# First norm of a decoder layer: POOL applies the norm's weights, VectorE the reciprocal column

## The chip, the cores and the metric

The kernel runs on one core of one Trainium2 chip. The metric is the device time in microseconds of that core, from runs of the whole program. The core's engines are called as in the profile: PE (TensorE), DVE (VectorE), ACT (ScalarE), POOL (GpSimd), and SP (SyncE), which issues all the DMAs here.

## What is computed

One layer of a decoder on 1024 tokens of width 1024 with 16 meta tokens in front (1040 rows in all), float32. Cut to what matters here:

```python
def rms_norm(x, g):
    y = xf * lax.rsqrt(jnp.mean(xf * xf, axis=-1, keepdims=True) + RMS_EPS)
    return (y * g.astype(jnp.float32)).astype(x.dtype)

mix = hybrid_mixer(rms_norm(h, g_mix_pre[l]), w_in[l], ...)
h = h + rms_norm(mix, g_mix_post[l])
ff = sq_relu_mlp(rms_norm(h, g_mlp_pre[l]), w_mlp_in[l], w_mlp_out[l])
h = h + rms_norm(ff, g_mlp_post[l])
```

The mixer projects the normalised rows with `w_in` and runs two kinds of attention on the result (stick-breaking attention and a sparse one in which an indexer picks 256 keys), gates and merges both, and projects out. The change concerns the first `rms_norm` alone, the one with `g_mix_pre`.

## The kernel before

All products of matrices are split: each operand is kept as a rounded part (`_hi`) and the rest (`_lo`), and three matmuls stand for one. The program has three blocks, one behind the other (the `nc.Block()` of lines 331, 506 and 1281). Each block holds a stream of instructions for every engine, and at its end all five engines meet in a barrier: nothing of the next block begins before all have arrived. The first block is the first norm, the second the projections and both attentions, the third the branches, the output projection and the MLP.

In the first block the 1040 rows are cut into nine tiles of 128 rows (`NT` is 9; the last has `LAST`, 16 rows). SP loads tile 0 of `x` (two DMAs), then the weights `g_bc` (one row, broadcast to 128 partitions), tile 1, the identity `idf`, and the other tiles, with the first two units of projection weights (`w_raw`) in between. For each tile c, with s = c % 2:

- ACT `first(c)` squares the tile with a sum per row (line 364, `junk1` and `small`) and, when DVE has made the variance, takes the square root (line 366).
- DVE `first(c)` makes the variance (line 388), the reciprocal of the root (line 390), and the normalised tile `xn[s]` (line 393), one SCALAR_TENSOR_TENSOR: `x` times the reciprocal column times `g_bc`. From tile 2 on it waits for the transposes of tile c - 2, which read the same half of `xn`. Ahead of everything DVE waits for `g_bc`.
- PE transposes `xn` in eight pieces into `tps[s]`, 128x128 each (line 419), when DVE has read the tile before last out of it.
- ACT `second(c)` rounds `tps` into `x_hi` (line 371), DVE `second(c)` subtracts that from `tps` into `x_lo` (line 399).

ACT and DVE both go `first(0)`, then `first(c)` and `second(c-1)` for c from 1 to 8, then `second(8)`; the order is written out by hand, and each engine executes in that order. ACT moreover casts the weight units 0 and 1 to `w_hi` (line 303) behind `second(4)` and `second(6)`. POOL does nothing in this block but `rest_unit` (line 307): `w_lo` from `w_raw` and `w_hi`, once for each of the two units. At the end DVE makes two small casts (lines 407, 408).

All sizes of `xn`, `xs`, `g_bc` and `x_lo` are 1024 columns of float32 per partition. The later blocks are named here only where a row comes from them: line 307 again (weights), line 630 and 639 (POOL, rests of projections and of transposed attention weights), lines 654 and 1345 (POOL, an addition of two tiles and `w_lo` in the third block), lines 1072, 1093 and 1102 (DVE, TENSOR_SCALARs of the search for the 256 keys), line 1119 (DVE, a product of two tiles), line 1578 (DVE, a square), line 683 (PE, the projections).

Of the kernel before, what the change touches and what calls it, by code (L numbers as in the profile page):

```python
# [16 lines left out]
F32, F32R, BF16, I32 = mybir.dt.float32, mybir.dt.float32r, mybir.dt.bfloat16, mybir.dt.int32  # L17
ALU, ACT = mybir.AluOpType, mybir.ActivationFunctionType
ds = bass.ds

P = 128
D = 1024
# [10 lines left out]
NT = -(-T // P)  # L33
# [147 lines left out]
for m_ in range(HI * NCH):  # L181
    n_, k_ = slots_[m_ * len(slots_) // (HI * NCH)]
# [48 lines left out]
O_SEL = O_XA + 2 * KT * T * 4  # L231
# [16 lines left out]
def build(nc, x, meta, w_units, b_gate, g_pre, g_post, g_mlp_pre, g_mlp_post, ident, strict, fill,  # L248
          rope_i, rope_d, out):
    with ExitStack() as ctx:  # L250
        def at(name, shape, dt, off):
            return nc.alloc_sbuf_tensor_at(name, shape, dt, offset=off)

        def sem(name):
            return ctx.enter_context(nc.semaphore(name))

        def psum(stack, name, shape):
            return stack.enter_context(nc.psum_tensor(name, shape, F32))
# [26 lines left out]
        small = at("small", [P, 512], F32, O_CONST + 2560)  # L285
# [14 lines left out]
        def round_unit(act, v, s, use):  # L300

            act.wait_ge(raw_landed[s], (use + 1) * 16)
            act.copy(w_hi[:, s], w_raw[:, s]).then_inc(hi_done, 1)  # L303

        def rest_unit(pool, v, s):
            pool.wait_ge(hi_done, v + 1)
            pool.tensor_tensor(w_lo[:, s], w_raw[:, s], w_hi[:, s].bitcast(F32), ALU.subtract).then_inc(lo_done, 1)  # L307
# [14 lines left out]
        xs = at("xs", [P, NT, D], F32, O_SEL)  # L322
        xn = at("xn", [P, 2, D], F32, O_SEL + NT * D * 4)
        g_bc = at("g_bc", [P, D], F32, O_SEL + NT * D * 4 + 8192)
        junk1 = at("junk1", [P, D], F32, O_SEL + NT * D * 4 + 12288)
        with ExitStack() as st:  # L326
            tps = [psum(st, f"n_tps{i}", [P, KT, P]) for i in range(2)]
            const_in, id_in, g_in, sq_done, var_done, std_done, r_done = (sem("n_" + n) for n in ("const", "id", "g", "sq", "var", "std", "r"))
            x_in = [sem(f"n_x{c}") for c in range(NT)]
            xn_done, t_done, h_done, l_done, cast_done = (sem("n_" + n) for n in ("xn", "t", "hi", "lo", "cast"))  # L330
            block = st.enter_context(nc.Block())

            def rows(c):
                return LAST if c == NT - 1 else P

            @block.sync
            def _(sp):
                def load_x(c):
                    if c == 0:
                        sp.dma_start(xs[0:META, 0], meta).then_inc(x_in[0], 16)  # L340
                        sp.dma_start(xs[META:P, 0], x[0:P - META, :]).then_inc(x_in[0], 16)
                    else:
                        sp.dma_start(xs[0:rows(c), c], x[c * P - META:c * P - META + rows(c), :]).then_inc(x_in[c], 16)

                load_x(0)
                sp.dma_start(g_bc[:], g_pre.broadcast_to([P, D])).then_inc(g_in, 16)
                load_x(1)
                sp.dma_start(idf[:], ident).then_inc(id_in, 16)
                for c in range(2, NT):
                    load_x(c)  # L350
                    if c in (3, 5):
                        v = (c - 3) // 2
                        sp.dma_start(w_raw[:, v], w_units[v * P:(v + 1) * P, :].rearrange("p (k n) -> p k n", k=KT)).then_inc(raw_landed[v], 16)
                for t, src in ((fill_f, fill), (strict_f, strict), (bg, b_gate)):
                    sp.dma_start(t[:], src).then_inc(const_in, 16)

            @block.scalar
            def _(act):
                act.activation(small[:, 30:31], nc.const_aps.tensor(1.0, (P, 1), F32), ACT.Sqrt)

                def first(c):
                    r, s = rows(c), c % 2
                    act.wait_ge(x_in[c], 32 if c == 0 else 16)
                    act.activation(junk1[0:r], xs[0:r, c], ACT.Square, accum_out=small[0:r, s:s + 1]).then_inc(sq_done, 1)
                    act.wait_ge(var_done, c + 1)
                    act.activation(small[0:r, 4 + s:5 + s], small[0:r, 2 + s:3 + s], ACT.Sqrt).then_inc(std_done, 1)

                def second(c):
                    r, s = rows(c), c % 2
                    act.wait_ge(t_done, c + 1)  # L370
                    act.copy(x_hi[:, :, c * P:c * P + r], tps[s][:, :, 0:r]).then_inc(h_done, 1)

                first(0)
                for c in range(1, NT):
                    first(c)
                    second(c - 1)
                    if c in (5, 7):
                        round_unit(act, (c - 5) // 2, (c - 5) // 2, 0)
                second(NT - 1)

            @block.vector
            def _(dve):
                dve.wait_ge(g_in, 16)

                def first(c):
                    r, s = rows(c), c % 2
                    dve.wait_ge(sq_done, c + 1)
                    dve.tensor_scalar(small[0:r, 2 + s:3 + s], small[0:r, s:s + 1], 1.0 / D, EPS, ALU.mult, ALU.add).then_inc(var_done, 1)
                    dve.wait_ge(std_done, c + 1)
                    dve.reciprocal(small[0:r, 6 + s:7 + s], small[0:r, 4 + s:5 + s]).then_inc(r_done, 1)  # L390
                    dve.wait_ge(r_done, c + 1)
                    dve.wait_ge(t_done, c - 1) if c >= 2 else None
                    dve.scalar_tensor_tensor(xn[0:r, s], xs[0:r, c], small[0:r, 6 + s:7 + s], g_bc[0:r], ALU.mult, ALU.mult).then_inc(xn_done, 1)

                def second(c):
                    r, s = rows(c), c % 2
                    cols = slice(c * P, c * P + r)
                    dve.wait_ge(h_done, c + 1)
                    dve.tensor_tensor(x_lo[:, :, cols], tps[s][:, :, 0:r], x_hi[:, :, cols].bitcast(F32), ALU.subtract).then_inc(l_done, 1)

                first(0)
                for c in range(1, NT):
                    first(c)
                    second(c - 1)
                second(NT - 1)
                dve.wait_ge(const_in, 48)
                dve.tensor_copy(strict_b[:], strict_f[:]).then_inc(cast_done, 1)
                dve.tensor_copy(idb[:], idf[:]).then_inc(cast_done, 1)

            @block.tensor  # L410
            def _(pe):
                pe.wait_ge(id_in, 16)
                for c in range(NT):
                    r, s = rows(c), c % 2
                    pe.wait_ge(xn_done, c + 1)
                    if c >= 2:
                        pe.wait_ge(l_done, c - 1)
                    for kt in range(KT):
                        mm = pe.transpose(tps[s][:, kt, 0:r], xn[0:r, s, kt * P:(kt + 1) * P], idf[0:r, 0:r])
                    mm.then_inc(t_done, 1)  # L420

            @block.gpsimd
            def _(pool):
                for v in range(2):
                    rest_unit(pool, v, v)

# [37 lines left out]
        with ExitStack() as st:  # L464
# [363 lines left out]
            def _(act):  # L828
# [30 lines left out]
                def relu(m):  # L859
                    _, c0, c1 = CH[m % NCH]  # L860
                    act.wait_ge(s_ready, m + 1)
                    if m >= 4:
                        act.wait_ge(s_acc, m - 3)
                    act.activation(relu_b[:, m % 4, 0:c1 - c0], bk[2 + m % 4][:, 0:c1 - c0], ACT.Relu).then_inc(s_relu, 1)
# [399 lines left out]
        with ExitStack() as st:  # L1264
# [14 lines left out]
            x_in = [sem("t_x0"), sem("t_x1")]  # L1279
# [400 lines left out]
```

## Time and profile before

| | us |
|---|---|
| median of 3 runs | 1809.07 (1806.93 to 1817.53) |
| profiled execution | 1808.41 |
| its span, first to last instruction | 1806.6 |
| PE busy | 1713.6 (95%) |
| DVE busy | 1009.9 (56%) |
| ACT busy | 690.9 (38%) |
| POOL busy | 546.0 (30%) |

The granted clock of TensorE is 0.99 of full speed over the whole span. A row of the timeline begins with the start and the duration in microseconds; an instruction that is held up after its issue shows the wait as part of its duration. In square brackets stands how long the engine was idle before, and what ended that.

### The profile page before, as it was taken

The page shows a single profiled execution, that of the slowest core. Times are in us where ns is not written, and L with a number is a line of the kernel's source. Part 1 is how long each engine was busy: PE and PEld are TensorE (multiplying, and loading weights), DVE is VectorE, ACT ScalarE, POOL GpSimd, SP SyncE. Part 2 cuts the span into 40 slices and gives each one's busy share as a digit, 9 for nine tenths or more (in the row PEclk, how much of TensorE's full clock was granted, in tenths as well). Part 3 has the DMA queues.
Part 4 walks back from the last instruction along what each step waited for, and adds up shares of the span by engine and source line. Part 5 has one row for each costly group of instructions (what it writes and reads, how often), then busy time and mean ns, then how long its engine had stood idle before and what let it go on. Part 6 is the DMA issues. An engine that isn't in the chain of part 4 may idle for free.

```text
span 1806.6 us, 22857 instructions
## 1 busy us (share of the span) xinstructions
PE 1713.6 (95%) x8744; PEld 1446.5 (80%) x8744; DVE 1009.9 (56%) x1626; ACT 690.9 (38%) x1356; POOL 546.0 (30%) x281
## 2 busy tenths in 40 slices
PE   5989999999999999888899999999999999999998
PEld 4889888899877777777778788888888888888886
DVE  5277798798898899678744344222222222222225
ACT  5366555554554544677621324111212020303032
POOL 1112255563443444211024501222223130404033
PEclk9999899999999999999999999999999999999999
DMA  4565424534424323644134431211111111202023
GB/s 169 159 176 158 124 91 128 148 97 113 120 71 110 113 87 93 144 106 108 41 140 152 175 117 71 70 36 58 47 47 49 46 59 35 74 20 82 12 86 136
DMA packets 67044, 174.56 MB, mean 97 GB/s; under 512 B 9256, under 2 KB 23912, under 8 KB 66936
## 3 DMA queue, kind: packets, MB, share of 16 engines
q1 hardware_dynamic: 66936, 173.10, 31.3%
q8 instruction: 70, 1.15, 0.3%
q14 instruction: 38, 0.31, 0.1%
HBM read 128.57 MB, written 44.50 MB: 96 GB/s over the span
## 4 chain that ended last, share of the span: by engine, by line
PE 47%; POOL 1%; DVE 1%; DMA 1%; ACT 0%; issue 0%; DVEq 0%
PE bank L1368 22%; PE bank L1393 19%; PE bank L317 5%; POOL row_lo L1345 1%; DMA w_raw<-w_units 1%; PE bank L1386 0%; DVE nn L1571 0%; POOL w_lo L307 0%; DVE scaled L1603 0%; DVE tt L1553 0%; ACT L1483 0%; DVE hh L1558 0%; DVE acc L1591 0%; DVE fin L1608 0%; DVE m_lo L1562 0%; ACT nn L1489 0%
## 5 line engine op out<-in xcount | busy, mean ns | idle before, releaser
L683 PE MATMUL bk<-x_hi,w_hi 128*128 128x512 f32 (+2 forms) x832 | 309.1, 372 | 1.2 <-PEq L326 1.2
L683 PE MATMUL bk<-x_lo,w_hi 128*128 128x512 f32 (+2 forms) x832 | 299.1, 360 | 0.0
L683 PE MATMUL bk<-x_hi,w_lo 128*128 128x512 f32 (+2 forms) x832 | 298.6, 359 | 0.0
L1496 ACT ACTIVATE relu<-bank 128x1024 f32<-128x1024 f32 x32 | 32.9, 1029 | 504.8 <-PE bank L1393 504.8
L1345 POOL TENSOR_TENSOR w_lo<-w_raw,w_hi 128x1024 fp32r<-128x1024 f32 x32 | 82.9, 2599 | 397.9 <-ACT w_hi L1460 397.9
L1393 PE MATMUL bank<-m_hi,w_hi 128*128 128x512 f32 x512 | 199.5, 390 | 0.0
L1393 PE MATMUL bank<-m_hi,w_lo 128*128 128x512 f32 x512 | 199.2, 389 | 0.0
L1393 PE MATMUL bank<-m_lo,w_hi 128*128 128x512 f32 x512 | 199.2, 389 | 0.0
L639 POOL TENSOR_TENSOR pt_lo<-a_buf,pt_hi 128x512 fp32r<-128x512 f32 (+3 forms) x104 | 138.3, 1347 | 193.0 <-ACT pt_hi L903 192.9
L307 POOL TENSOR_TENSOR w_lo<-w_raw,w_hi 128x1024 fp32r<-128x1024 f32 x53 | 130.4, 2461 | 191.6 <-ACT w_hi L303 191.4
L1060 DVE TENSOR_SCALAR_CACHE_REDUCE counted<-sc,small 128x272 uint8<-128x272 f32 (+6 forms) x217 | 182.4, 890 | 0.9
L1591 DVE TENSOR_TENSOR acc<-acc,bank 128x1024 f32<-128x1024 f32 x56 | 68.4, 1221 | 192.5 <-PE bank L1368 191.7
L683 PEld LDWEIGHTS bk<-x_hi,w_lo 128*128 128x128 f32 x832 | 158.6, 191 | 17.6
L683 PEld LDWEIGHTS bk<-x_hi,w_hi 128*128 128x128 f32 x832 | 159.1, 191 | 16.0 <-issue 1.3
L683 PEld LDWEIGHTS bk<-x_lo,w_hi 128*128 128x128 f32 x832 | 159.1, 191 | 13.5
L1578 DVE TENSOR_TENSOR sq<-relu 128x1024 f32<-128x1024 f32 x32 | 39.2, 1225 | 227.9 <-ACT relu L1496 227.9
L783 PE MATMUL bk<-pt_hi,v_hl 128*128 128x256 f32 (+2 forms) x384 | 110.9, 313 | 10.6 <-ACT o_st L922 5.8
L1393 PEld LDWEIGHTS bank<-m_hi,w_lo 128*128 128x128 f32 x512 | 96.1, 188 | 20.0
L1393 PEld LDWEIGHTS bank<-m_lo,w_hi 128*128 128x128 f32 x512 | 96.1, 188 | 19.9
L1393 PEld LDWEIGHTS bank<-m_hi,w_hi 128*128 128x128 f32 x512 | 96.1, 188 | 19.8
L748 PE MATMUL bk<-idf,a_buf 128*128 128x128 f32 (+1 forms) x704 | 100.3, 277 | 4.1 <-DVE pt_lo L1165 2.5
L1116 DVE TENSOR_TENSOR_SCAN n_buf<-n_buf 128x1040 f32<-128x1040 f32 (+3 forms) x64 | 101.8, 1591 | 2.3 <-ACT n_buf L879 2.3
(187 smaller groups left out, 3461.7 us busy)
## 6 DMA issues: line engine op xcount, KB each, us to landing
w_raw<-w_units SPq DMA_DIRECT2D x99, 512.0 KB, 3.6
raw<-w_units SPq DMA_DIRECT2D x24, 512.0 KB, 3.3
k_hi<-k_d SPq DMA_DIRECT2D x32, 260.0 KB, 5.7
k_lo<-k_d SPq DMA_DIRECT2D x32, 260.0 KB, 6.2
q_st<-q_d SPq DMA_DIRECT2D x32, 256.0 KB, 4.9
g_d<-stage_hi SPq DMA_DIRECT2D x32, 256.0 KB
gate<-g_d SPq DMA_DIRECT2D x16, 512.0 KB, 4.5
qi<-iq_d SPq DMA_DIRECT2D x32, 128.0 KB, 3.1
```

The costliest lines, as they stand in the source:

```text
L307: pool.tensor_tensor(w_lo[:, s], w_raw[:, s], w_hi[:, s].bitcast(F32), ALU.subtract).then_inc(lo_done, 1)
L317: mm = pe.matmul(o, w[:, s, kt, :], a[:, a_of(kt), c0:c1], start=(kt == kts[0] and n == 0), stop=(kt == kts[-1] and n == 2))
L639: pool.tensor_tensor(pt_of(pt_lo, j, tiles), raw, pt_of(pt_hi, j, tiles).bitcast(F32), ALU.subtract).then_inc(sb_lo, 1)
L683: mm = pe.matmul(pj[b][:, 0:c1 - c0], w[:, s, kt, :], a[:, kt, c0:c1], start=kt == 0 and k == 0, stop=kt == KT - 1 and k == 2)
L748: mm = pe.transpose(bk[TP_BANK[n]][0:r, m * P:(m + 1) * P], a_buf[:, j % 3, col:col + r], idf[:])
L783: mm = pe.matmul(dst, v_hl[0:r, g % 2, slot, :], w[0:r, cols], start=slot == 0 and w is hi, stop=slot == o + 1 and w is lo)
L1060: op(dve.tensor_scalar(counted[:, blk(b)], sc[:, blk(b)], cand[:, j:j + 1], None, ALU.is_ge, ALU.add, accum_out=cnt[:, j:j + 1]))
L1116: dve.tensor_tensor_scan(n[:, ::-1], n[:, ::-1], n[:, ::-1], 1.0, ALU.mult, ALU.bypass).then_inc(scan_done, 1)
L1345: pool.tensor_tensor(unit_lo(v), raw_ring[(v - V0) % 3], unit_hi(v).bitcast(F32), ALU.subtract).then_inc(lo_done, 1)
L1368: mm = pe.matmul(ps[:, c * HALF:(c + 1) * HALF], a[:, cols], w[:, c * HALF:(c + 1) * HALF], start=first and n == 0, stop=last and n == 2)
L1393: mm = pe.matmul(m1_ps[n][:, c * HALF:(c + 1) * HALF], w[s][:, kt, :], a[:, kt, c * HALF:(c + 1) * HALF], start=kt == 0 and i == 0, stop=k ...
L1591: dve.tensor_tensor(acc[:, t], acc[:, t], m2_ps[g][:], ALU.add).then_inc(acc_done, 1)
```

## The change

POOL gets a new instruction per tile: `xg[c % 3] = x[c] * g_bc`, into a ring of three buffers of 128x1024 that lies behind `junk1`. It waits for `g_bc` once, for the tile's load, and from tile 3 on for DVE's `xn` of tile c - 3, which reads the same buffer. DVE's product becomes a TENSOR_SCALAR, `xg` times the reciprocal column; it waits for POOL's product besides what it waited for, and DVE no longer waits for `g_bc`. POOL's two `rest_unit` stand behind its nine products.

```diff
@@ -323,11 +323,12 @@
+        xg = at("xg", [P, 3, D], F32, O_SEL + NT * D * 4 + 16384)
...
-            xn_done, t_done, h_done, l_done, cast_done = (sem("n_" + n) for n in ("xn", "t", "hi", "lo", "cast"))
+            xg_done, xn_done, t_done, h_done, l_done, cast_done = (sem("n_" + n) for n in ("xg", "xn", "t", "hi", "lo", "cast"))
@@ -380,8 +381,6 @@
             @block.vector
             def _(dve):
-                dve.wait_ge(g_in, 16)
-
                 def first(c):
@@ -389,8 +388,9 @@
                     dve.wait_ge(r_done, c + 1)
+                    dve.wait_ge(xg_done, c + 1)
                     dve.wait_ge(t_done, c - 1) if c >= 2 else None
-                    dve.scalar_tensor_tensor(xn[0:r, s], xs[0:r, c], small[0:r, 6 + s:7 + s], g_bc[0:r], ALU.mult, ALU.mult).then_inc(xn_done, 1)
+                    dve.tensor_scalar(xn[0:r, s], xg[0:r, c % 3], small[0:r, 6 + s:7 + s], None, ALU.mult).then_inc(xn_done, 1)
@@ -421,6 +421,13 @@
             @block.gpsimd
             def _(pool):
+                pool.wait_ge(g_in, 16)
+                for c in range(NT):
+                    r = rows(c)
+                    pool.wait_ge(x_in[c], 32 if c == 0 else 16)
+                    if c >= 3:
+                        pool.wait_ge(xn_done, c - 2)
+                    pool.tensor_tensor(xg[0:r, c % 3], xs[0:r, c], g_bc[0:r], ALU.mult).then_inc(xg_done, 1)
                 for v in range(2):
                     rest_unit(pool, v, v)
```

POOL's instructions in the first block, before (`n_...` and `hi_done` are semaphores; `n_x0` to `n_x8` count the loads of `x`, `n_g` that of `g_bc`, `n_xn` DVE's products):

```order
L422 UNCONDITIONAL_BRANCH [waits barrier_Pool_Activation_PE_DVE_SP_gather]
L307 ISA
L307 TENSOR_TENSOR w_lo<-w_raw,w_hi 128x1024 [waits hi_done] x2
L326 UNCONDITIONAL_BRANCH
L623 UNCONDITIONAL_BRANCH [waits barrier_Pool_Activation_PE_DVE_SP_gather]
```

and of the changed kernel:

```order
L430 ISA
L430 TENSOR_TENSOR xg<-xs,g_bc 128x1024 [waits n_x0,n_g]
L430 TENSOR_TENSOR xg<-xs,g_bc 128x1024 [waits n_x1]
L430 TENSOR_TENSOR xg<-xs,g_bc 128x1024 [waits n_x2]
L430 TENSOR_TENSOR xg<-xs,g_bc 128x1024 [waits n_xn,n_x3]
L430 TENSOR_TENSOR xg<-xs,g_bc 128x1024 [waits n_xn,n_x4]
L430 TENSOR_TENSOR xg<-xs,g_bc 128x1024 [waits n_xn,n_x5]
L430 TENSOR_TENSOR xg<-xs,g_bc 128x1024 [waits n_xn,n_x6]
L430 TENSOR_TENSOR xg<-xs,g_bc 128x1024 [waits n_xn,n_x7]
L430 TENSOR_TENSOR xg<-xs,g_bc 16x1024 [waits n_xn,n_x8]
L307 TENSOR_TENSOR w_lo<-w_raw,w_hi 128x1024 [waits hi_done] x2
```

Nine products now stand ahead of the two `w_lo`; the one-off set-up (`ISA`) has moved to the first of them.

DVE's first instructions of the block, before (`n_sq` counts ACT's sums, `n_std` its roots, `n_r` the reciprocals, `n_hi` the rounded tiles):

```order
L388 TENSOR_SCALAR small<-small 128x1 [waits n_sq,n_g]
L390 RECIPROCAL small<-small 128x1 [waits n_std]
L393 SCALAR_TENSOR_TENSOR xn<-xs,small,g_bc 128x1024 [waits n_r]
L388 TENSOR_SCALAR small<-small 128x1 [waits n_sq]
L390 RECIPROCAL small<-small 128x1 [waits n_std]
L393 SCALAR_TENSOR_TENSOR xn<-xs,small,g_bc 128x1024 [waits n_r]
L399 TENSOR_TENSOR x_lo<-n_tps,x_hi 128x8x128 [waits n_hi]
```

and of the changed kernel (`n_xg` counts POOL's products):

```order
L387 TENSOR_SCALAR small<-small 128x1 [waits n_sq]
L389 RECIPROCAL small<-small 128x1 [waits n_std]
L393 TENSOR_SCALAR xn<-xg,small 128x1024 [waits n_xg,n_r]
L387 TENSOR_SCALAR small<-small 128x1 [waits n_sq]
L389 RECIPROCAL small<-small 128x1 [waits n_std]
L393 TENSOR_SCALAR xn<-xg,small 128x1024 [waits n_xg,n_r]
L399 TENSOR_TENSOR x_lo<-n_tps,x_hi 128x8x128 [waits n_hi]
```

The order on DVE is the same; the wait for the weights has gone from the first instruction, and each product waits for POOL's.

## Rows read from the trace of the kernel before

**Rows 1.** Stretches: PE, PEld, DVE, ACT, POOL busy (count); granted clock, DMA share, GB/s.

```profile
38.54:1806.60 1768.06, 1696.90 (x8672) 1433.00 (x8672) 984.94 (x1588) 668.01 (x1316) 541.06 (x275) 0.99 0.31 95
```

**Rows 2.** Who waited for whom from 0 to 45 us: total, times, longest.

```profile
PE n_tps L419 <- DVE xn L393: 20.6, 9, 9.0
```

**Rows 3.** Timeline, the start of the stage: start us, duration us, engine, line.

```profile
6.98 0.15 DVE L388 TENSOR_SCALAR small<-small 128x1 f32<-128x1 f32 x1 [6.98 <-DMA g_bc<-g_pre]
...
7.61 1.28 DVE L393 SCALAR_TENSOR_TENSOR xn<-xs,small,g_bc 128x1024 f32<-128x1024 f32 x1
...
8.30 1.06 ACT L364 ACTIVATE junk<-xs 128x1024 f32<-128x1024 f32 x1 [0.92 <-DMA xs<-x]
```

**Rows 4.** Timeline, from `xn` of tile 3 to `xn` of tile 5.

```profile
16.76 1.28 DVE L393 SCALAR_TENSOR_TENSOR xn<-xs,small,g_bc 128x1024 f32<-128x1024 f32 x1
...
18.10 1.97 PE L419 MATMUL n_tps<-idf,xn 128*128 128x128 f32 x8 [0.98 <-DVE xn L393]
...
19.95 1.28 DVE L393 SCALAR_TENSOR_TENSOR xn<-xs,small,g_bc 128x1024 f32<-128x1024 f32 x1
...
21.15 1.22 DVE L399 TENSOR_TENSOR x_lo<-n_tps,x_hi 128x1024 fp32r<-128x1024 f32 x1
...
22.90 1.28 DVE L393 SCALAR_TENSOR_TENSOR xn<-xs,small,g_bc 128x1024 f32<-128x1024 f32 x1
```

**Rows 5.** Timeline, the stage's second part, where POOL works too.

```profile
24.34 1.23 DVE L399 TENSOR_TENSOR x_lo<-n_tps,x_hi 128x1024 fp32r<-128x1024 f32 x1 [0.16 <-ACT x_hi L371]
...
25.34 2.35 POOL L307 TENSOR_TENSOR w_lo<-w_raw,w_hi 128x1024 fp32r<-128x1024 f32 x1 [24.89 <-ACT w_hi L303]
...
26.34 0.15 DVE L388 TENSOR_SCALAR small<-small 128x1 f32<-128x1 f32 x1 [0.77 <-ACT junk L364]
...
26.96 1.81 DVE L393 SCALAR_TENSOR_TENSOR xn<-xs,small,g_bc 128x1024 f32<-128x1024 f32 x1
...
30.43 1.28 DVE L393 SCALAR_TENSOR_TENSOR xn<-xs,small,g_bc 128x1024 f32<-128x1024 f32 x1
...
34.46 1.83 DVE L393 SCALAR_TENSOR_TENSOR xn<-xs,small,g_bc 16x1024 f32<-16x1024 f32 x1
...
37.71 0.29 DVE L399 TENSOR_TENSOR x_lo<-n_tps,x_hi 128x128 fp32r<-128x128 f32 x1 [0.29 <-ACT x_hi L371]
```

**Rows 6.** Prices elsewhere: DVE line 1072 by shape; POOL line 654, ns min/median/max.

```profile
L1072 DVE TENSOR_SCALAR sc<-sc,small 128x1040 f32<-128x1040 f32 x1 | 0.8, 752 | 0.0
...
L654 POOL TENSOR_TENSOR o_raw<-o_raw,o_raw x4: 2362/2374/2379, 748.9 to 835.6; 128x1024 f32<-128x1024 f32 x4
```

**Rows 7.** Timeline of the search: two TENSOR_SCALARs and the POOL instructions they met.

```profile
675.61 3.14 POOL L307 TENSOR_TENSOR w_lo<-w_raw,w_hi 128x1024 fp32r<-128x1024 f32 x1
676.51 2.65 DVE L1102 TENSOR_SCALAR sc<-sel_tmp 128x784 f32<-128x784 f32 x1
...
696.99 3.02 POOL L639 TENSOR_TENSOR pt_lo<-a_buf,pt_hi 128x512 fp32r<-128x512 f32 x2 [2.31 <-ACT pt_hi L903]
...
698.78 1.79 DVE L1093 TENSOR_SCALAR sel_tmp<-sel_tmp,small 128x1040 f32<-128x1040 f32 x1
```

**Rows 8.** Timeline: both engines wait at 241 to 244; POOL waits for VectorE at 1200.

```profile
241.47 3.06 DVE L1119 TENSOR_TENSOR a_buf<-a_buf,n_buf 128x784 f32<-128x784 f32 x1
...
241.30 2.40 POOL L307 TENSOR_TENSOR w_lo<-w_raw,w_hi 128x1024 fp32r<-128x1024 f32 x1 [4.36 <-ACT w_hi L303]
243.64 1.75 POOL L639 TENSOR_TENSOR pt_lo<-a_buf,pt_hi 128x384 fp32r<-128x384 f32 x1
...
1198.86 1.23 DVE L1578 TENSOR_TENSOR sq<-relu 128x1024 f32<-128x1024 f32 x1 [10.72 <-ACT relu L1496]
1199.84 2.51 POOL L1345 TENSOR_TENSOR w_lo<-w_raw,w_hi 128x1024 fp32r<-128x1024 f32 x1 [49.83 <-ACT w_hi L1460]
```

**Rows 9.** Busy time by stretch, columns as in rows 1: the second block's first matmuls.

```profile
38.50:44.20 5.70, 5.61 (x19) 5.64 (x20) 0.00 (x0) 0.00 (x0) 0.00 (x0) 1.00 0.78 274
44.20:46.00 1.80, 1.80 (x12) 1.80 (x12) 0.00 (x0) 0.69 (x2) 0.00 (x0) 1.00 0.06 25
```

## The prediction

> **What bounds the kernel now.** I read the table of stretches first. The stage that the change touches, the first norm, lasts from the start to 38.54 us. In the 1768.06 us behind it TensorE is busy for 1696.90, 96% [rows 1]. All five engines leave the stage through a barrier, and all later work starts behind that, so I take a change of the stage's length to pass to the total one for one: TensorE is the limit there and nothing in it waits for a time of day. The whole stage is 2% of the span; no edit to it can move the total by much, and 1% (18 us, about what a measurement of this kernel can tell from no change) is half the stage.
>
> Next the waits of that stretch: TensorE waited 20.6 us for `xn`, the product that is changed [rows 2]. So the path goes through VectorE. Then the timeline. At the start VectorE waits for the weights `g_bc` (6.98) and multiplies tile 0 at 7.61 [rows 3]. In the steady part the tiles run as two chains, even and odd ones. The odd chain in [rows 4]: `xn` of tile 3 at 16.76, its transposes at 18.10, ScalarE's rounding behind them, VectorE's `x_lo` at 21.15, and, behind the small work for the reciprocal, `xn` of tile 5 at 22.90. That is 6.14 us for two tiles, 3.07 per tile. Without the multiplication itself (1.28) it is 22.90 - 18.04 = 4.86 us from the end of one `xn` to the moment when the next of that chain can start.
>
> **What the change removes.** Nine products of 1.28 us on VectorE become nine TENSOR_SCALARs with one tile as input. The same form with a column as factor stands in the later search: 128x1040 in 0.752 us [rows 6], so about 0.74 for 1024 columns. If only that counted, 0.54 us would go from each two-tile chain, 0.27 per tile, some 2.2 us over eight tiles.
>
> **What it adds.** Nine POOL multiplications 128x1024 (the last with 16 partitions, as long, since length goes by columns: VectorE's `xn` of 16 partitions took 1.83, that of 128 under the same conditions 1.81 [rows 5]). The trace has no POOL multiplication. Its additions of the same shape and type took 2.362 to 2.379 us [rows 6], and I take 2.37. Bounds: from 2.0 (a multiplication somewhat cheaper than an addition) to 3.0, between the addition and the 3.14 of a subtraction that was held up [rows 7]. POOL is idle in the stage before, save for two `w_lo` of 2.35, so its 21.3 us of work have room; what matters is when it runs and whom it blocks.
>
> **What it collides with.** In the stage of before `xn` of tile 6 took 1.81 instead of 1.28 where it met POOL's `w_lo`: POOL ended at 25.34 + 2.35 = 27.69, VectorE at 28.77, 1.08 later. Tile 8 paid the same [rows 5]. The new form does this too: the TENSOR_SCALAR of 676.51 had to take 0.6 and took 2.65; POOL ended at 678.75, VectorE at 679.16. With 1040 columns, the one at 698.78 ended at 700.57, 0.56 after POOL (700.01) [rows 7]. So a `xn` that meets a running multiplication stands still until POOL is through and then needs 0.55 us. Instructions that read PSUM do not: `x_lo` at 24.34 ran over POOL's start at 25.34 with neither longer, and the small L388 at 26.34 (0.15) under POOL neither [rows 5].
>
> Who gets on when both wait? At 241.30 POOL ran a `w_lo` until 243.70 and had its next instruction issued at 243.64; VectorE had been waiting since 241.47. VectorE went first (it ended at 244.53, 0.83 after the release, the length of 784 columns), and POOL's 128x384 ended at 245.39, having taken 1.75. Behind VectorE's product that ended at 1200.09, POOL's 128x1024 ended at 1202.35, 2.26 later [rows 8]. So the two take turns, at 0.56 + 2.27 = 2.83 us per tile. The Trainium skill says so too (SBUF — State Buffer, section "Who interferes with whom"): a VectorE instruction in a mode that uses both port pairs, as a float32 `tensor_scalar` can be, and a GpSimd instruction exclude each other for their whole length. Its advice, to put the contended work off the critical path, speaks against this change: the product is on the path, and its feeder now holds it up. The trace agrees with the exclusion; on the turn when both queue, the page is silent.
>
> **The sum, tile by tile** (ends of `xn`):
> - Tile 0. POOL: 6.98 to 9.35. It issues the next at 9.30 (0.06 before an end, as at 243.64; x of tile 1 is there, ScalarE reads it at 8.30 [rows 3]). VectorE, told of the product, asks at 9.39, 0.09 late, and waits for the whole second multiplication: until 11.67, end 12.22. Before: 8.89. So +3.3.
> - Tile 1. The third multiplication runs 12.22 to 14.49. `xn` is asked for at about 12.8, waits, and ends at 15.04.
> - Tiles 2 to 5: one every 2.83, so tile 5 ends at 12.22 + 5 x 2.83 = 26.37. Before: 22.90 + 1.28 = 24.18. So +2.2; 1.1 of 3.3 has come back. The two-tile chain would allow it: 2 x 2.83 - 0.55 = 5.11 is more than 4.86.
> - Tile 6. ScalarE casts a weight in between, so it is asked for 26.96 - 21.23 = 5.73 after tile 4's end (23.54), at 29.27 (21.23 is 1.28 behind the start at 19.95 [rows 4]). Behind tile 5's end POOL makes its eighth multiplication until 28.64 and goes straight on with the last, until 30.97, since nothing is queued against it at that moment; `xn` waits for it and ends at 31.52. Before 28.77: +2.75. POOL's `w_lo` of unit 0 queues behind it, to 33.79.
> - Tile 7: asked for 1.66 after tile 6's end (30.43 - 28.77), at 33.18, waits for `w_lo`, ends 34.34. Before 31.71: +2.6.
> - Tile 8: asked for 5.69 after tile 6's end, 37.21. The second `w_lo` starts about 35.6 (its cast follows the rounding of tile 6), ends about 38.0; `xn` ends 38.55. Before 34.46 + 1.83 = 36.29: +2.3. The last `x_lo` moves from 37.71 [rows 5] to 40.0, and with it the barrier.
>
> The profiled execution took 1808.41 us (span 1806.6 and 1.8 around it), 0.7 below the median of the three runs, 1809.07. It gives 1810.7 with +2.3, the median 1811.4. I take 1811.0.
>
> **What is left uncertain in it.** Each 0.1 us on POOL's multiplication moves eight turns, some 0.8 us. With 2.6 it is +4; with 2.2 or less the two-tile chain takes over at (4.86 + 0.55)/2 = 2.7 per tile, and it is +1 to +2. TensorE's rate in the next stage is another term: its first matmuls there took 5.61 us for 19, 0.295 each; those behind 44.2 us 1.80 for 12, 0.15 each, of the same shape, while the granted clock reads 1.00 in both stretches [rows 9]. So 19 matmuls cost 0.145 more, some 2.8 us in all. Whether that stretch stays as long when the stage before it has other gaps, no row tells; I take no change, and -2.8 to +2.8 as its ends.
>
> **Rivals.**
> 1. *No exclusion in this pairing: faster.* If `xn` did not stand still beside POOL's multiplication, tile 0 would end at 9.39 + 0.74 = 10.13 (+1.2), and each pair of tiles would take 6.14 - 0.54 = 5.60. Over eight tiles that is -2.2, and tiles 6 and 8 lose the 0.5 that they wait for `w_lo` now: about -1.8 in all, 1807. It decides as soon as `xn` takes 0.74 rather than 0.9 or more at tiles 2 to 5. For it: the sharing is in the trace only with POOL subtractions and additions. Against it: both TENSOR_SCALARs that started while POOL ran stood until POOL's end, and so did a product of two tiles (241.47) [rows 7, 8]. 0.12.
> 2. *POOL goes on first whenever both queue.* Then three multiplications run before tile 0 (end 14.0, `xn` 14.5, +5.6), the ring is full, and each turn has the semaphore's 0.04 and an unshortened 2.37: 2.96. With the two `w_lo` also ahead, tile 8 ends near 41.6: +5.3, 1813.9. For it: POOL issues back to back. Against: the turn at 243.70. 0.12.
> 3. *A POOL multiplication is slower than an addition.* At 3.0 us, 0.63 more in nine turns: +2.3 + 5.7 = +8, 1816. No row speaks for or against. 0.08.
> 4. *TensorE's slower stretch moves* by up to its whole length: 1808.2 or 1813.8. 0.08.
>
> **How the numbers follow.** The forecast has 0.60. The range for 8 in 10 reaches from rival 1 (1807) to short of rival 3: 1807 to 1815.5; three runs of the kernel before lie 10 us apart, so the high side is left wide. A difference above 18 us is reached by no case: faster 0.01, slower 0.02, within 1% 0.97.
>
> **What would show it.** In the changed kernel's timeline: `xn` of tile 0 with about 2.8 us instead of 0.74; `xn` of tiles 2 to 5 with 0.8 to 0.9, ending 2.8 apart; POOL's multiplications with 2.4 twice and then about 2.9, back to back; the last `x_lo` near 40. Wrong: `xn` at 0.74 throughout (rival 1); three multiplications ahead of the first `xn` (rival 2); POOL rows of 3 us with nothing before them (rival 3); a stage that is longer and a total that isn't, or the reverse (rival 4).

## The result and the profile after

| | before | after |
|---|---|---|
| median | 1809.9 us (22 runs, 1805.25 to 1817.53) | 1817.79 us (22 runs, 1810.07 to 1823.57) |
| ratio to before | | 1.0040, 95% interval 1.0027 to 1.0054 |
| ratio in a second comparison (12 runs, with other kernels beside it) | | 1.0021, interval 1.0005 to 1.0036 |
| profiled execution, span | 1808.41, 1806.6 | 1814.99, 1813.1 |
| start of the second block | 38.59 | 43.71 |

The changed kernel is slower, by 0.4% in the first comparison and 0.2% in the second. The forecast was 1811.0 with a range to 1815.5: the sign was right, the size too small by more than half, and the median lies outside the range. The first block, where the change is, takes 5.12 us longer; 2.3 had been worked out.

The timeline of the changed kernel's first block, VectorE's product `xn`, tile by tile (start us, duration us; tiles 0, 1, 2, 3, 6, 7 and 8). These are the rows that answer to [rows 3 to 5]:

```profile
9.35 2.73 DVE L393 TENSOR_SCALAR xn<-xg,small 128x1024 f32<-128x1024 f32 x1 [2.26 <-POOL xg L430]
...
12.62 2.23 DVE L393 TENSOR_SCALAR xn<-xg,small 128x1024 f32<-128x1024 f32 x1
...
17.01 2.91 DVE L393 TENSOR_SCALAR xn<-xg,small 128x1024 f32<-128x1024 f32 x1
...
21.58 1.39 DVE L393 TENSOR_SCALAR xn<-xg,small 128x1024 f32<-128x1024 f32 x1
...
31.74 2.68 DVE L393 TENSOR_SCALAR xn<-xg,small 128x1024 f32<-128x1024 f32 x1
...
36.09 0.75 DVE L393 TENSOR_SCALAR xn<-xg,small 128x1024 f32<-128x1024 f32 x1
...
40.11 1.30 DVE L393 TENSOR_SCALAR xn<-xg,small 16x1024 f32<-16x1024 f32 x1
```

Tile 7 shows the price of the new form with nothing in its way: 0.75, where [rows 3] have 1.28. All others wait in place. The first two are as forecast (9.39 and 2.83; 12.8, end 15.04). Tile 2 is where the run leaves the forecast: it took 2.91, to 19.92, not to 17.9. POOL's rows of the same stretch (its products of tiles 2, 3, 4, 5 and 8, then the first `w_lo`) say why:

```profile
11.49 2.80 POOL L430 TENSOR_TENSOR xg<-xs,g_bc 128x1024 f32<-128x1024 f32 x1
14.26 2.81 POOL L430 TENSOR_TENSOR xg<-xs,g_bc 128x1024 f32<-128x1024 f32 x1
17.02 2.34 POOL L430 TENSOR_TENSOR xg<-xs,g_bc 128x1024 f32<-128x1024 f32 x1
...
20.06 2.36 POOL L430 TENSOR_TENSOR xg<-xs,g_bc 128x1024 f32<-128x1024 f32 x1 [0.70 <-DVE xn L393]
...
29.22 2.35 POOL L430 TENSOR_TENSOR xg<-xs,g_bc 16x1024 f32<-16x1024 f32 x1 [0.69 <-DVE xn L393]
31.54 2.33 POOL L307 TENSOR_TENSOR w_lo<-w_raw,w_hi 128x1024 fp32r<-128x1024 f32 x1
```

The products of tiles 2 and 3 took 2.80: 0.04 until the product before them was through, 0.55 for the `xn` in front, then 2.21 of their own. The next was issued at 17.02, `xn` of tile 2 at 17.01, and the product that both waited for ended at 17.07. POOL went on, and `xn` waited for all of it. This near miss is called the race of tile 2 below. With that product POOL had filled three buffers and could not issue the next product until `xn` had freed one: the rows from 20.06 on begin 0.14 behind an `xn`'s end, after 0.7 of idleness. From there a tile costs 3.05 (20.06, 23.11, 26.16), the pace of before, and none of the late start comes back. Last, `w_lo` went in at 31.54, 0.20 ahead of `xn` of tile 6, which cost that tile 1.9 us more than the 0.75 of a free product. The waits of the first 45 us carry the sum; the first answers to [rows 2] (20.6 there):

```profile
PE n_tps L419 <- DVE xn L393: 25.7, 9, 12.2
...
POOL xg L430 <- DVE xn L393: 2.8, 4, 0.7
DVE small L389 <- ACT small L367: 2.4, 9, 0.3
DVE xn L393 <- POOL xg L430: 2.3, 1, 2.3
```

TensorE waits 5.1 us longer for `xn`. VectorE waited for POOL's result itself only once, for tile 0; the rest of its loss is inside the durations above, where no view of waits shows it.

### The profile page after: what moved, and what is told of

It reads as the page before. It is cut to its first block, busy times and chain, and to the rows that moved or that the text cites. A ratio compares the mean times of both kernels' runs of the same rounds, so it can differ in the third digit from the quotient of the medians.

```text
span 1813.1 us, 22874 instructions
## 1 busy us (share of the span) xinstructions
PE 1713.8 (95%) x8744; PEld 1446.4 (80%) x8744; DVE 1013.6 (56%) x1626; ACT 690.8 (38%) x1356; POOL 568.1 (31%) x290
## 4 chain that ended last, share of the span: by engine, by line
PE 47%; POOL 1%; DVE 1%; DMA 1%; ACT 0%; issue 0%; DVEq 0%
PE bank L1375 22%; PE bank L1400 19%; PE bank L317 5%; POOL row_lo L1352 1%; DMA w_raw<-w_units 1%; PE bank L1393 0%; DVE nn L1578 0%; POOL w_lo L307 0%; DVE tt L1560 0%; DVE scaled L1610 0%; ACT L1490 0%; DVE hh L1565 0%; DVE acc L1598 0%; DVE m_lo L1569 0%; DVE fin L1615 0%; ACT nn L1496 0%
```

## Experiments

Theory A was what the rows above suggest: the loss is the exclusion between POOL's product and VectorE's, and its size depends on who is in front at each turn. Theory B, the rival: POOL as a feeder is too slow or too late, and the exclusion is a side show. Most runs are one profile each; what is compared is the start of the second block (TensorE's first matmul there), which repeats (43.71 and 43.52 for the changed kernel in two sessions, 41.74 and 41.81, 40.92 and 40.99, 39.25 and 39.12 for three of the others), while totals move by 10 us.

### Fewer buffers, and more

```diff
...
-        xg = at("xg", [P, 3, D], F32, O_SEL + NT * D * 4 + 16384)
+        xg = at("xg", [P, 1, D], F32, O_SEL + NT * D * 4 + 16384)
...
-                    if c >= 3:
-                        pool.wait_ge(xn_done, c - 2)
+                    if c >= 1:
+                        pool.wait_ge(xn_done, c - 0)
```

> One buffer instead of three: POOL starts a product only when xn of the tile before is through. Theory A (the loss comes from POOL going ahead and holding xn up, made worse by the race lost at tile 2): with one buffer POOL can't be in front of a waiting xn, so xn takes 0.75 at tiles 0 to 5, a tile costs 2.34 + 0.75 + 0.08 = 3.17, and the second block starts at 40.5, 3.2 us before that of the changed kernel (43.7), though the overlap is less. Rival B (POOL's throughput as a feeder is the limit, the exclusion is a side show): fewer buffers can only cost; the second block starts at 43.7 or later, up to 9 x 3.17 behind the start, no earlier than after.

The second block started at 41.74, 2.0 earlier than with three buffers. The timeline of VectorE and POOL at tiles 3 and 8, with the second `w_lo` in a row of its own:

```profile
19.43 0.75 DVE L393 TENSOR_SCALAR xn<-xg,small 128x1024 f32<-128x1024 f32 x1 [0.97 <-POOL xg L430]
...
36.17 2.82 DVE L393 TENSOR_SCALAR xn<-xg,small 16x1024 f32<-16x1024 f32 x1 [0.28 <-POOL xg L430]
...
38.34 2.86 POOL L307 TENSOR_TENSOR w_lo<-w_raw,w_hi 128x1024 fp32r<-128x1024 f32 x1
```

`xn` took 0.75 at tiles 0 to 7, and a tile cost 3.35 (3.17 expected: each handing over by semaphore took 0.11 to 0.14, not the 0.04 that I had put in). At the end the two `w_lo` and the last `xn` met, as the 2.82 shows. The last `w_lo` ended at 41.20, and VectorE's small cast of line 407 stood behind it (0.67 us, 0.22 before). Both the longer turn and this meeting make it 41.74 instead of 40.5. Theory B is wrong here: a third of the buffers and less overlap gave a shorter stage. Timed later, it came to a ratio of 1.0015:

> The kernel with one buffer again, timed in rounds. Its second block started at 41.74, 3.15 after that of before and 1.97 before that of the changed kernel, so the total is 3.2 us over before (0.17%), if the stage is all that differs; the clock of the later stages moves single runs by up to 10 us either way.

Measured 1813.44 against 1809.72 (12 and 23 runs), ratio 1.0015, interval 1.0001 to 1.0029; 3.2 us are 1.0018.

With nine buffers and no wait:

> Nine buffers, no wait of POOL for VectorE at all. Theory A: POOL still goes first where xn is asked for a hair late, so some xn take 2.9 and the second block starts at 43 to 44.5, no better than with three buffers (only if the race at tile 2 is won by chance, 40.6). Rival B: with its waits gone (0.7 before each product from tile 5 on) POOL delivers sooner; the second block starts near 41 or earlier.

It started at 42.75, 0.25 under A's range, far from B's 41, and 1.0 before the changed kernel. `xn` of tile 2 lost the race again, at 17.07 against POOL's 17.09, and from there the two took turns, as I had forecast for three buffers:

```profile
17.07 2.93 DVE L393 TENSOR_SCALAR xn<-xg,small 128x1024 f32<-128x1024 f32 x1
...
21.66 1.10 DVE L393 TENSOR_SCALAR xn<-xg,small 128x1024 f32<-128x1024 f32 x1
...
24.86 0.75 DVE L393 TENSOR_SCALAR xn<-xg,small 128x1024 f32<-128x1024 f32 x1
```

So the full ring costs about 1 us of the 5.1; the late start of tile 0, the lost race and `w_lo` make the rest. POOL's waits alone, as in B, do not explain it.

### One wait more

```diff
                     if c >= 3:
-                        pool.wait_ge(xn_done, c - 2)
+                        pool.wait_ge(xn_done, 3 if c == 4 else c - 2)
```

> Three buffers, and one wait more: POOL's product of tile 4 waits for xn of tile 2. Theory A: the race of 17.0 us goes the other way, xn of tile 2 takes 0.75 instead of 2.9 and ends near 17.8 (19.92 after); what follows can lose a race elsewhere, so the second block starts between 40.4 and 41.9, 2 to 3 us earlier, by one added wait. Rival B: an added wait can only delay POOL: 43.7 or later.

It started at 40.92, 2.8 earlier. VectorE's row for tile 2:

```profile
17.09 0.75 DVE L393 TENSOR_SCALAR xn<-xg,small 128x1024 f32<-128x1024 f32 x1
```

An added wait on one POOL instruction gave back more than half of the stage's loss. This is the sharpest test of the race: all instructions and buffers are the same. What is left against before is 2.33 us, the 2.3 of the forecast's sum, and it comes about tile by tile as forecast: `xn` of tile 6 waited for POOL's last product (2.25 at 29.38; 29.27 and 2.25 forecast) and that of tile 8 ended at 38.62 (38.55 forecast). Timed:

> One wait more at tile 4, as in the earlier run (second block at 40.92). Stage alone: 2.3 us over before, ratio 1.0013, and 2.8 under the changed kernel beside it. Rival C: 5 over before.

1811.6 us, ratio 1.0009, interval 0.9993 to 1.0025: not told apart from before.

### A slower product that holds nothing up

```diff
-                    dve.tensor_scalar(xn[0:r, s], xg[0:r, c % 3], small[0:r, 6 + s:7 + s], None, ALU.mult).then_inc(xn_done, 1)
+                    dve.tensor_scalar(xn[0:r, s], xg[0:r, c % 3], small[0:r, 6 + s:7 + s], None, ALU.mult, ALU.add,
+                                      accum_out=small[0:r, 8 + s:9 + s]).then_inc(xn_done, 1)
```

> VectorE's product also writes a sum to an unused column, the form that ran at POOL's side unstretched in the search. Everything else as in the changed kernel. Theory A: xn takes 1.27 to 1.35 at all nine tiles though its own work has nearly doubled, POOL's products 2.34 to 2.36 each with none at 2.8; the second block starts at 39.8, 3.9 us earlier than with the form that takes 0.75. Rival B: xn is slower by 0.5 and POOL as before: 43.7 or later.

Start 39.25, 4.5 earlier than the changed kernel. By line, over all nine tiles (ns min/median/max):

```profile
L431 POOL TENSOR_TENSOR xg<-xs,g_bc x9: 2342/2357/2375, 7.1 to 26.3; 128x1024 f32<-128x1024 f32 x8, 16x1024 f32<-16x1024 f32 x1
...
L393 DVE TENSOR_SCALAR_CACHE_REDUCE xn<-xg,small x9: 1268/1279/1280, 9.6 to 35.7; 128x1024 f32<-128x1024 f32 x8, 16x1024 f32<-16x1024 f32 x1
```

Neither engine shows a single stretched instruction. VectorE's own work on the product went from 0.75 to 1.28 and the stage got shorter. That settles that the exclusion, and not POOL's speed or the dependency, makes the loss. The Trainium skill has both halves (SBUF — State Buffer, section "Who interferes with whom"): a `tensor_scalar` can take the shared ports, "not the form that also writes out its accumulator". The trace agrees: 1.27 to 1.28 at every tile, beside POOL products of 2.34 to 2.38. Timed:

> The product in the form with a sum (second block at 39.25 in the earlier run). Stage alone: 0.7 us over before, ratio 1.0004, no difference that can be told; rival C, where it is POOL's added work or its heat that costs the later blocks: 3 to 4 over before.

1809.34 us, ratio 0.9993, interval 0.9977 to 1.0008, that is 4.2 us less to 1.4 more than before. The stage's 0.7 is inside, the 3 to 4 of rival C are not: POOL's nine products cost the later blocks nothing that this comparison can tell.

### The two halves apart

VectorE's half: `xn` from `x` itself, POOL's products gone; the norm's weights are left out.

> VectorE's half alone: xn is x times the reciprocal column; POOL makes no products, and the norm's weights are left out of the result. Theory A: 0.75 at most tiles, 1.2 at the two that meet w_lo; the second block starts at 36.6, 2.0 earlier than before (38.59). So the shorter form by itself is worth 2 us, and POOL's half costs 7 (36.6 to 43.7). Rival B agrees on this run; a start at 38 or later would say that VectorE's product was never on the path.

Start 35.66, 2.9 earlier than before. (0.9 earlier than estimated; the product of tile 4 came 2.45 behind that of tile 3, where it came 3.19 behind before.) VectorE's first wait for the weights is gone here too, but `xn` of tile 1 was issued at 10.15, 10.10 before, so the 2.9 are not that wait's. The shorter form is on the path and pays.

POOL's half, into buffers that nobody reads, with VectorE's old product:

```diff
...
+                pool.wait_ge(g_in, 16)
+                for c in range(NT):
+                    r = rows(c)
+                    pool.wait_ge(x_in[c], 32 if c == 0 else 16)
+                    pool.tensor_tensor(xg[0:r, c], xs[0:r, c], g_bc[0:r], ALU.mult).then_inc(xg_done, 1)
```

> POOL's half alone, into nine buffers that nobody reads; VectorE does its old product from x, with its old waits, and waits for POOL nowhere. Theory A: xn takes 1.6 to 3.2 instead of 1.28, POOL's products 3.3 instead of 2.35 where they wait in turn, and the second block starts near 43.8, as late as with the whole change, without any dependency on POOL's products. Rival B (the change loses because VectorE must wait for POOL's result): with no such wait the second block starts as before, 38.6 to 39.5.

Start 43.75, as late as with the whole change, without one wait of VectorE for POOL. A product and a POOL row in turn:

```profile
18.68 1.64 DVE L394 SCALAR_TENSOR_TENSOR xn<-xs,small,g_bc 128x1024 f32<-128x1024 f32 x1
...
19.20 3.35 POOL L429 TENSOR_TENSOR xg<-xs,g_bc 128x1024 f32<-128x1024 f32 x1
```

The 3.35 is 0.04 until POOL's own product before it was through, the 1.08 of VectorE's product in front [rows 5], and 2.23. The halves are worth -2.9 and +5.2; the whole came to +5.1, so nothing is left of the short form's gain where POOL works beside it.

### A version without the product

VectorE multiplies the identity by the column, 128 columns instead of 1024, and TensorE multiplies POOL's tile by that diagonal where it transposed before.

```diff
...
-                    dve.wait_ge(xg_done, c + 1)
+                    dve.wait_ge(id_in, 16)
...
-                    dve.tensor_scalar(xn[0:r, s], xg[0:r, c % 3], small[0:r, 6 + s:7 + s], None, ALU.mult).then_inc(xn_done, 1)
+                    dve.tensor_scalar(dg[0:r, s], idf[0:r], small[0:r, 6 + s:7 + s], None, ALU.mult, ALU.add,
+                                      accum_out=small[0:r, 8 + s:9 + s]).then_inc(xn_done, 1)
...
-                        mm = pe.transpose(tps[s][:, kt, 0:r], xn[0:r, s, kt * P:(kt + 1) * P], idf[0:r, 0:r])
+                        mm = pe.matmul(tps[s][:, kt, 0:r], xg[0:r, c % 3, kt * P:(kt + 1) * P], dg[0:r, s, 0:r], start=True, stop=True)
...
-                        pool.wait_ge(xn_done, c - 2)
+                        pool.wait_ge(t_done, c - 2)
```

> The reciprocal goes through TensorE: VectorE multiplies the 128x128 identity by the column (in the form that writes a sum too), and PE multiplies POOL's x*g by that diagonal instead of transposing with the identity; xn is gone. Theory A: nothing on VectorE contends with POOL any more, POOL's nine products take 2.35 each, VectorE's new one 0.3 to 0.4; a tile costs about 2.75 (ScalarE's turn), and the second block starts at 34.6, 4.0 before that of the kernel before and 9 before that of the changed one; total 4 us (0.2%) under before. If PE's products with the diagonal cost more than the transposes (1.97 for eight), later by twice the difference per two tiles. Rival B (POOL's 9 x 2.35 as the limit): 6.9 + 21.2 is 28.1 for the last product, so it would not bind here either; it says nothing against 34.6.

1808.11 against 1809.72 us, ratio 0.9983, interval 0.9968 to 0.9999: the only kernel here whose interval lies under before, by a hair. The second block started at 37.31, 1.3 before that of before, not 4. The timeline of TensorE's first product and of a later one:

```profile
9.43 5.46 PE L422 MATMUL n_tps<-dg,xg 128*128 128x128 f32 x24 [9.43 <-POOL xg L433]
13.22 1.01 ACT L373 CAST x_hi<-n_tps 128x1024 fp32r<-128x1024 f32 x1 [3.46 <-PE n_tps L422]
...
28.02 2.05 PE L422 MATMUL n_tps<-dg,xg 128*128 128x128 f32 x16 [1.27 <-DVE dg L394]
```

A tile's eight products appear as 16 matmuls. Later tiles took 2.05, close to the 1.97 of [rows 4], but tile 0 lasted from 9.43 to ScalarE's start at 13.22, 3.8 us, and the last tile 1.95 instead of 1.03. These two ends, 1.8 and 0.9, add up to the 2.7 that are missing. At the start a matmul took 0.23 (5.46 for 24), later 0.13 (2.05 for 16), nearly the ratio of the two stretches of [rows 9]; so tile 0 is a matter of TensorE's rate there, which this run didn't test. The contention itself is gone, as expected: POOL's products took 2.34 to 2.37.

### The changed kernel again

> The changed kernel itself, timed beside the next two. If the stage is all that the change costs (theory A with the totals), it is 5.1 us over before (second block at 43.71 instead of 38.59), ratio 1.0028. If the change also makes the later blocks slower (rival C: the first comparison gave 7.9 us, 2.8 more than the stage), it is 7 to 8 over, 1.004 or more.

1816.48 against 1810.07 us (12 and 29 runs), ratio 1.0021, interval 1.0005 to 1.0036: the stage's 1.0028 is inside, 1.004 is not. The first comparison's interval starts at 1.0027, so it holds the stage's figure too, at its edge. A cost in the later blocks is not needed to explain the total; that there is none of a microsecond or so is not shown.

## Why the prediction was wrong, by its own steps

- **The path and the prices.** Right. A later start of the second block carried through to the total as far as the intervals can tell. A pair of traces with the same stretches of half clock shows it plainly: the run with one wait more was 2.33 behind before at the second block's start and 2.47 at 907 us (last section). POOL's product: 2.34 to 2.36, forecast 2.37. The new form: 0.75, forecast 0.74. Behind a release: 0.55, as read from [rows 7].
- **Tiles 0 and 1.** Right to 0.2 us: 12.08 and 14.85 measured as ends, 12.22 and 15.04 forecast.
- **"Tiles 2 to 5: one every 2.83 ... The two-tile chain would allow it: 2 x 2.83 - 0.55 = 5.11 is more than 4.86."** This is the step that failed. The margin of 0.25 was taken as safe. The turn was 2.77 rather than 2.83 (2.22 for POOL behind a release, 0.55 for VectorE), which takes 0.12 from it over two turns, and the chain took 4.93 from the end of tile 0 (12.08) to the request of tile 2 (17.01) rather than 4.86. What was left is 0.06 before POOL's release at 17.07, and POOL's own next instruction is issued 0.05 before its end. I had noted that early issue for tile 0 and not applied it here. The lost race put 2.1 us on tile 2's end: 19.92, where the forecast's sum gives 17.88 and the run with one wait more ended it at 17.84. That run took away this race alone and came to the forecast's +2.3 instead of +5.1; so the 2.8 us between them hang on this step.
- **What follows a lost race.** Not in the prediction at all: that POOL, once a product ahead, runs into its ring's end, then starts each product only on `xn`'s end and costs 3.05 per tile. Rival 2 had this state and its price (2.96 per tile, +5.3, 1813.9), but as a rule of who goes first from tile 0 on, with 0.12. Its state came about by the timing of one instruction. The +5.3 is close to the 5.1 measured; the reason given for it was not the right one, since at tiles 0 and 1 VectorE went ahead of POOL's next product.
- **Tiles 6 to 8.** `w_lo` was put behind `xn` of tile 6; with `xn` of that tile issued 2.4 later than in the run with one wait more it came 0.20 before it, 2.68 instead of 2.25 for that tile.
- **The range.** Its high side was set by rival 3 and ended short of the 1816 that this gave. The measured median would have been outside even so. Of the 7.1 us from 1810.7, the profile's own sum, to the median, 2.8 are the stage's, 1.5 what the profiled execution has beyond the stage (what is left of clock terms of both signs, see the last section), and 2.8 the distance from that execution to the median of its kernel.
- **Rivals 1 and 3** fell: in the changed kernel no `xn` that met a POOL product ran at 0.75, and POOL's products had the price of additions. **Rival 4**, that TensorE's slower stretch moves, was real: it is in the last section, with other stretches like it.

## What to carry to other kernels

Before half of an operation goes to GpSimd, look whether what stays on VectorE and what moves can run at the same time: here the short form, which has to take turns with POOL, gained nothing, and the form with 1.28 us beat the one with 0.75. Where two engines exclude each other and one of them can issue ahead, a ring of buffers lets it take the turn at a near miss; here one buffer, or one wait in the right place, cost less. A schedule worked out from rows with margins of some 0.1 us holds until the first near miss; give both orders a price, and a chance.

## What was not expected of the hardware

- **Who goes first.** Issued at 17.01 (VectorE) and 17.02 (POOL) before a release at 17.07, and at 17.07 and 17.09 in the run with nine buffers, POOL went first. Where VectorE had asked 0.09 us or more ahead of POOL's issue, VectorE went first: with nine buffers `xn` of tile 4 was issued at 24.86 and POOL's next product at 24.95, with one wait more `xn` of tile 5 at 25.75 and POOL's at 25.85, and both times `xn` took 0.75 and POOL 2.88. The second runs of the changed kernel and of that with one wait more gave the same turns. No run here shows, for this pair, a lead between 0.02 and 0.09.

  The prediction calls the Trainium skill silent on this. It is not: the same section (SBUF — State Buffer, "Who interferes with whom") has "Issue order, not op shape, decides who blocks." The rows agree where the lead is 0.09 or more; at the 0.01 and 0.02 of this pair the starts in the profile go against it.

  An estimate that fits all of them: each instruction has a stretch at its start that need not wait. For VectorE it is 0.75 - 0.55 = 0.20, for POOL 2.35 - 2.21 = 0.14, so VectorE's TENSOR_SCALAR would need a lead of more than 0.06. In its favour, the `xn` of 24.86 and 25.75 were issued 0.12 and 0.14 before POOL's running product ended, and still took 0.75. No run tests it, and it is for this pair of forms alone. A scan of the search, issued 0.01 ahead of POOL's subtraction, went first in the trace of before: it took 1.24, as it does without POOL, and the subtraction 1.95 instead of 0.93.

```profile
395.79 1.24 DVE L1116 TENSOR_TENSOR_SCAN n_buf<-n_buf 128x528 f32<-128x528 f32 x1
395.80 1.95 POOL L630 TENSOR_TENSOR stage_lo<-stage_lo,stage_hi 128x344 fp32r<-128x344 f32 x1
```

- **TensorE at the second block's start.** The matmuls of 0.49 us that [rows 9] show lasted 5.9 us before and 3.8 after, and for the same kernel 5.9 in one run and 3.0 in another (the form with a sum). In both of these the granted clock reads 0.50 there, 1.2 GHz, for matmuls of the same 0.49 us, so the 1.00 of [rows 9] is most likely a gap in the records. The two runs of that kernel, by stretch, columns as in rows 1:

```profile
39.20:45.10 5.90, 5.85 (x20) 5.88 (x21) 0.00 (x0) 0.00 (x0) 0.00 (x0) 0.50 0.76 267
```

```profile
39.10:42.10 3.00, 2.98 (x10) 3.00 (x11) 0.00 (x0) 0.00 (x0) 0.00 (x0) 0.50 0.67 187
```

- **A drop of the clock in the middle.** In the profiled run of the changed kernel TensorE was granted 0.50 from 909 on, across the start of the third block, and the first pair of matmuls of that block took 1.19 where it took 0.70 before. The first run with a sum had it too (912 to 924). The runs with one and nine buffers and the first with one wait more did not, but the second with one wait more read 0.50 from 909 to 918, and the run without POOL's products 0.50 from 905 to 909. So the drop comes and goes with one and the same kernel:

```profile
909.00:918.00 9.00, 7.81 (x29) 6.57 (x28) 3.19 (x5) 0.80 (x3) 0.00 (x0) 0.50 0.04 10
918.00:924.00 6.00, 6.00 (x21) 4.75 (x20) 1.23 (x1) 0.97 (x1) 0.00 (x0) 0.73 0.97 377
```

  What it cost shows where one and the same group of TensorE's instructions is set beside that of before. Before, the changed kernel, and the first run with one wait more:

```profile
906.78 1.09 PE L758 MATMUL bk<-idf,r_wide 128*128 128x128 f32 x8 [1.51 <-ACT r_wide L931]
```

```profile
907.48 1.90 PE L765 MATMUL bk<-idf,r_wide 128*128 128x128 f32 x8 [1.50 <-ACT r_wide L938]
```

```profile
909.25 1.10 PE L765 MATMUL bk<-idf,r_wide 128*128 128x128 f32 x8 [1.51 <-ACT r_wide L938]
```

  The changed kernel was 5.1 behind at the second block's start and only 0.7 behind here, since its stretches at half clock were shorter or fell elsewhere: 3.8 us against 5.9 at the block's start, and from 884 to 891 it was granted 1.00 where before was granted 0.51 (the two windows below, columns as in rows 1, before first). Then the drop put it 6.2 behind by 920, and there it stayed to within 0.3 of the span's +6.5. So that +6.5 lies near the stage's +5.1 is partly luck: some 4.4 us were given back and 5.5 taken by the clock. The run with one wait more had its stretches where before had them and kept its 2.3 to 2.5 throughout; the first run with a sum, 0.7 behind at the second block's start, ended 10.3 behind (span 1816.9).

```profile
884.00:891.00 7.00, 7.00 (x32) 6.24 (x30) 4.50 (x13) 3.06 (x8) 0.00 (x0) 0.51 0.01 2
```

```profile
884.00:891.00 7.00, 4.94 (x33) 4.04 (x32) 5.81 (x18) 4.52 (x12) 0.00 (x0) 1.00 0.01 2
```

  Over the 22 runs of after the mean granted clock goes from 0.982 to 0.992 and the time roughly from 1823 to 1811 with it. Whether the change makes such drops likelier is open.
